# One core, a four-half-layer decoder step in split fp32: parts of the inner dimension, the order around the residual, the mean square and the block sums

## The reference, cut to what matters

```python
def rms_norm(x, g):
    y = x * lax.rsqrt(jnp.mean(x * x, axis=-1, keepdims=True) + EPS)
    return y * g

def swiglu_ffn(x, w_in, w_out):            # w_in 1024 x 5632, w_out 2816 x 1024
    gate, up = jnp.split(x @ w_in, 2, axis=-1)
    return (jax.nn.silu(gate) * up) @ w_out

for l in range(2):
    if l == 1:
        kv = rms_norm(x, kv_norm) @ w_kv   # keys (rotated) and values, kept for the attention
    x = x + 0.5 * swiglu_ffn(rms_norm(x, norm_ffn[l, 0]), ffn_w_in[l, 0], ffn_w_out[l, 0])
    h = rms_norm(x, norm_mix[l])
    mix = conv_module(h, ...) if l == 0 else diff_attention(rope(h @ w_q), ...) @ w_o
    x = x + mix
    x = x + 0.5 * swiglu_ffn(rms_norm(x, norm_ffn[l, 1]), ffn_w_in[l, 1], ffn_w_out[l, 1])
y = rms_norm(x, norm_final)
```

## Time and profile before

| | us |
|---|---|
| median of 3 runs | 2050.07 |
| the profiled execution | 2052.34 |
| its span | 2050.5 |
| TensorE matmuls (PE) busy | 1940.7 |
| VectorE (DVE) busy | 1431.8 |
| ScalarE (ACT) busy | 874.0 |
| GpSimd (POOL) busy | 332.7 |

### The profile page before, as it was taken

How to read it: one execution, slowest core, us unless ns; L and a number is a source line. 1 busy time by engine, 2 the same in 40 slices (tenths; PEclk the granted TensorE clock), 3 DMA queues, 4 the chain that set the end, 5 groups by cost and what they waited for, 6 DMA issues and landing times. The chain is left out here.

```text
span 2050.5 us, 36491 instructions
## 1 busy us (share of the span) xinstructions
PE 1940.7 (95%) x15236; PEld 1859.0 (91%) x15236; DVE 1431.8 (70%) x1775; ACT 874.0 (43%) x1259; POOL 332.7 (16%) x343
## 2 busy tenths in 40 slices
PE   4999999999798999999998999999988989999997
PEld 3999999888598999999998999999875789999996
DVE  6776768699857758667655847667678567667585
ACT  5433424455545425234234424334356454334242
POOL 1101011133111011011411111011431121011111
PEclk9999999999899999999998999999999999999998
DMA  9768585388448487682549677673677167686752
GB/s 272 166 174 224 137 216 129 88 160 170 96 144 194 117 222 168 189 192 78 151 150 225 165 190 190 166 191 103 183 230 247 45 152 188 168 205 152 204 142 64
DMA packets 318784, 340.71 MB, mean 166 GB/s; under 512 B 12163, under 2 KB 279812, under 8 KB 318476
## 3 DMA queue, kind: packets, MB, share of 16 engines
q1 hardware_dynamic: 275460, 216.97, 33.7%
q0 software_dynamic: 33840, 111.21, 28.8%
q10 hardware_dynamic: 9320, 10.20, 1.7%
HBM read 221.58 MB, written 7.53 MB: 112 GB/s over the span
## 5 line engine op out<-in xcount | busy, mean ns | idle before, releaser
L682 PE MATMUL ps_all<-xs_hi_low,w_hi 128*128 128x260 f32 x1848 | 530.4, 287 | 36.0 <-DVE w_lo L1418 21.3
L682 PE MATMUL ps_all<-xs_hi_low,w_lo 128*128 128x260 f32 x1848 | 529.0, 286 | 0.0
L682 PE MATMUL ps_all<-xs_lo_low,w_hi 128*128 128x260 f32 x1848 | 526.3, 285 | 0.0
L1017 ACT ACTIVATE w_hi<-raw 128x1024 fp32r<-128x1024 f32 (+1 forms) x252 | 259.1, 1029 | 390.1 <-PE ps_all L652 132.2
L1418 DVE TENSOR_TENSOR w_lo<-raw,w_hi 128x1024 fp32r<-128x1024 f32 (+1 forms) x252 | 311.7, 1237 | 129.9 <-ACT w_hi L1017 126.7
L682 PEld LDWEIGHTS ps_all<-xs_hi_low,w_hi 128*128 128x128 f32 x1848 | 354.3, 192 | 38.4 <-issue 25.7
L682 PEld LDWEIGHTS ps_all<-xs_lo_low,w_hi 128*128 128x128 f32 x1848 | 353.9, 191 | 0.2
L682 PEld LDWEIGHTS ps_all<-xs_hi_low,w_lo 128*128 128x128 f32 x1848 | 353.4, 191 | 0.0
L1017 ACT ACTIVATE w_hi<-raw_more_low 128x1024 fp32r<-128x1024 f32 x156 | 165.2, 1059 | 290.1 <-PE ps_all L682 184.0
L1418 DVE TENSOR_TENSOR w_lo<-raw_more_low,w_hi 128x1024 fp32r<-128x1024 f32 x156 | 192.0, 1231 | 118.4 <-ACT w_hi L1017 117.1
L652 PE MATMUL ps_all<-hs_hi_low,w_hi 128*128 128x260 f32 x1056 | 215.4, 284 | 2.8 <-DVE t_gate L1489 2.6
(11 more groups left out here) (254 smaller groups left out, 3612.2 us busy)
## 6 DMA issues: line engine op xcount, KB each, us to landing
raw_more_low<-w_in SPq DMA_DIRECT2D x105, 512.0 KB, 7.1
raw<-w_in SPq DMA_DIRECT2D x80, 512.0 KB, 6.0
raw_more_low<-raw_more_low POOLq DMA_DIRECT2D x72, 512.0 KB, 6.4
raw<-w_out SPq DMA_DIRECT2D x64, 512.0 KB, 4.2
raw<-raw POOLq DMA_DIRECT2D x60, 512.0 KB, 6.8
raw_more_high<-w_in SPq DMA_DIRECT2D x34, 512.0 KB, 6.9
raw<-w_out SPq DMA_DIRECT2D x32, 384.0 KB, 3.4
raw_more_high<-raw_more_high POOLq DMA_DIRECT2D x24, 512.0 KB, 6.7
```

The lines of the kernel that those rows point to most:

```text
L682: mm = nc.tensor.matmul(ps_all[:, bank, 0:HALF], w[:, ring, j * GW + q * P:j * GW + (q + 1) * P], m, start=j == 0 and k == 0, stop=j == PA ...
L1017: nc.scalar.activation(w_hi[:, n % RING, 0:width], src, ACT.Copy).then_inc(hi_made, 1)
```

## The change

Six things are changed.

1. `PARTS` is (6, 8, 8): the first part of each block has 3 groups and 6-tile chunks, the last one 4 groups and 8-tile chunks.
2. In the residual phases the weights of item n + 3 are made at the end of chunk n (`step(n + 1)`) and not at the start of the next one. Where pair sums are made (conv_out and o) VectorE drains x ahead of the rest of the pair before, and ScalarE squares an even tile first of all, rounds the next weights, and only then copies; at an odd tile it copies, rounds the next weights, then rounds the pair and squares.
3. The mean square of an up phase stands ahead of item 5, on banks 6 and 7, its root and refinement follow, and its result is awaited ahead of item 0 of group 1.
4. `add_pairs` adds S1 + W22 first, then S3 + W11; first loads come in the order W11, W12, S1, W22, S3.
5. In the first group of f 2 the blocks S1 and S3 have places of their own, like W12, and so wait for no free place.
6. At the start of the kernel all five blocks are loaded ahead of the constants.

```diff
-PARTS = (8, 8, 6)
-PART_AT = (0, 8, 16)
+PARTS = (6, 8, 8)
+PART_AT = (0, 6, 14)
...
-        ps_stat_up = ps_all[:, 0:2, 0:HALF]
+        ps_stat_up = ps_all[:, 6:8, 0:HALF]
...
-                for blk in (W11, W12, S3, S1, W22) if first_in else (S3, S1, W22, W11, W12):
+                for blk in (W11, W12, S1, W22, S3) if first_in else (S3, S1, W22, W11, W12):
                     s = blk + 5 * in_second(ph, g)
+                    apart = ph.f == 2 and ph.part == 0 and g == 0 and blk in APART
+                    after = 0 if apart else need[s]
...
+                    elif i == 0 and g == 1 and fresh(ph):
+                        pe.wait_ge(rstd_made, made + 1)
...
                     elif i == 5:
                         pe.wait_ge(p1_copied, ph.group0 + g + 1)
-                        if g == 0 and fresh(ph):
-                            pe.wait_ge(rstd_made, made + 1)
...
-                            if i == 3 and g == 0 and fresh(ph):
-                                variance(sums, (p1_copied, ph.group0 + 1), ps_stat_up)
+                            if i == 5 and g == 0 and fresh(ph):
+                                variance(sums, (taken, sums_of(ph, g, 3)), ps_stat_up)
...
@@ scalar, residual
+                    def square():
+                        act.wait_ge(summed, sums + m - 1)
+                        nc.scalar.activation(sq[:, m % 2, :], at(x, m), ACT.Square).then_inc(squared, 1)
+                    def following():
+                        if m < KD - 1:
+                            step(ph.chunk0 + m + 1)
...
-                        pair_hi(s, m)
...
+                        if m % 2 == 0:
+                            square()
+                            following()
+                            pair_hi(s, m)
+                        else:
+                            copy_x(s, m)
+                            following()
+                            pair_combos(s, m)
+                            square()
...
@@ vector, up
-                    if g == 0 and fresh(ph):
-                        rms(ps_stat_up)
                     thirds(g)
                     step(n + 5)
                     up_second(g)
...
+                    if g == 0 and fresh(ph):
+                        rms(ps_stat_up)
                     step(n + 6)
...
@@ vector, residual
-                    step(n)
-                    if s in (2, 6):
-                        pair_before_lo(s, m)
+                    if m == 0 or not ph.final:
+                        step(n)
...
                     if s in (2, 6):
-                        pair_sums(s, m)
+                        pair_before_lo(s, m)
+                        if m % 2:
+                            pair_sums(s, m)
+                        if m < KD - 1:
+                            step(n + 1)
+                        if m % 2 == 0:
+                            pair_sums(s, m)
+                        pair_lo(s, m)
...
@@ gpsimd
-                for to, of, done in ((S3, W11, s3_added), (S1, W22, s1_added)):
+                for to, of, done in ((S1, W22, s1_added), (S3, W11, s3_added)):
```

More of the change, by code:

```diff
@@ L262, in trunk @@
         stage_2, = over(XG + 108160, KD * T * 4, [("stage_2", [P, 8, HALF])])
-        w12_first, = over(XG + 62464, KD * P * 4, [("w12_first", [P, KD * P])])
+        first_places = over(XG + 54144, 3 * KD * P * 4, [(f"first_block{i}", [P, KD * P]) for i in range(3)])
         def stage_of(s, j):
@@ L394, in trunk @@
         W11, S1, W22, S3, W12 = range(5)
+        APART = {S1: 0, S3: 1, W12: 2}
         BLOCK_OF = (W11, W12, S3, W11, S1, W22, W12)
@@ L404, in trunk @@
                 first_in = ph.group0 + g == 0 or ph.kind == "up" and ph.f == 2 and ph.part == 0 and g == 0
-                for blk in (W11, W12, S3, S1, W22) if first_in else (S3, S1, W22, W11, W12):
+                for blk in (W11, W12, S1, W22, S3) if first_in else (S3, S1, W22, W11, W12):
                     s = blk + 5 * in_second(ph, g)
+                    apart = ph.f == 2 and ph.part == 0 and g == 0 and blk in APART
+                    after = 0 if apart else need[s]
+                    if not apart:
+                        need[s] = ph.chunk0 + ITEMS * g + FREED_BY[blk] + 1
+                    elif blk != W12:
+                        s = 10 + APART[blk]
                     filled[s] += 16
@@ L409, in trunk @@
                     a, b = {W11: (0, 0), W12: (0, 1), W22: (1, 1), S1: (1, 0), S3: (1, 0)}[blk]
-                    of_phase.append((s, need[s], ph.weights(g, a, b), g, blk))
-                    need[s] = ph.chunk0 + ITEMS * g + FREED_BY[blk] + 1
+                    of_phase.append((s, after, ph.weights(g, a, b), g, blk))
             for c in range(ph.chunks):
@@ L440, in block_of @@
         def block_of(ph, g, block):
-            if ph.f == 2 and ph.part == 0 and g == 0 and block == W12:
-                return w12_first[:, :]
+            if ph.f == 2 and ph.part == 0 and g == 0 and block in APART:
+                return first_places[APART[block]][:, :]
             return raw_of(ph, block + 5 * in_second(ph, g))
@@ L572, in _ @@
                 sp.dma_start(x[:, 2 * i:2 * i + 2, :], xT[:, 2 * i:2 * i + 2, :]).then_inc(x_in[i], 16)
-                if i < 3:
-                    load(first, i)
+                load(first, i)
+            load(first, 4)
             sp.dma_start(cst[:, :], cst_d).then_inc(inputs, 16)
@@ L577, in _ @@
             sp.dma_start(pages_s[0:1, :], pages).then_inc(inputs, 16)
-            load(first, 3)
-            load(first, 4)
             for m in range(4):
@@ L1146, in up @@
                             hidden_hi(g - 1)
-                        elif not g and i == 3 and fresh(ph):
+                        elif not g and i == 5 and fresh(ph):
                             root(ps_stat_up)
@@ L1185, in residual @@
                         continue
-                    step(ph.chunk0 + m)
-                    act.wait_ge(summed, sums + m - 1)
+                    if m == 0:
+                        step(ph.chunk0)
                     if ph.kind == "down":
```

33 lines of the change are left out of this document (16 added, 17 removed).

## The result

The changed kernel takes 2001.37 us (median, 1999.82 to 2003.08) against 2050.39 before: ratio 0.9766, 95% interval 0.9749 to 0.9783. Timed again beside later kernels it took 1999.99 us, ratio 0.9756 (0.9743 to 0.9769). So 49 us are won; the prediction was 2000, with a sum of 50.3 us against the profiled execution.

What follows compares the result with a forecast made beforehand. PE, busy 1940.7 of 2050.5 us, was taken as the bound, so only its waits and half clock could be won. Terms summed to 50.3 us off the profiled 2052.3, giving 2002.0, or 2000 us as median; range 1992 to 2013.

Steps and rivals of the forecast that it cites:

- Last down phases: Last down phases of f 0, f 1, f 2: 8-tile chunks make PE the bound, 2.7 us each, 8.1 us won.
- The ring of 5.21 us: Last down phase before: VectorE and ScalarE loop through x, copy, square, w_hi, w_lo, drain, against 4.3 us of PE.
- Squares earlier: k, q and conv_in: wait for summed squares and half clock go, 4.7 us each in k and q, 4.2 in conv_in; 13.6.
- Order in conv_out and o: New order makes PE bound the pair loop, 11.5 us for 14.11; 9.4 and 9.0 us, together 18.4.
- Mean square behind item 4: First group of f 1 and f 3: rstd wait and half clock go, 0.3 us wait stays; 3.65 each, 7.3 us.
- f 0: First group of f 0: item 5 starts behind the mean square at 48.3, not 51.36; 2 us, between -1 and 5.
- Block sums: Reordered sums, f 2's first group and later groups: item 2 needing the second sum costs 0, between -2 and 2 us.
- Tail: Kernel's end: last half chunk covers 0.7 us more of the mean square's wait, chunk 7 overlaps better; 1.4 us won.
- Even-group starts: Down phases behind a group of even count start with a 0.2 us gap, f 2 has two more; -0.5 us.
- signs of being wrong: Mean square waiting over 1 us, a pair above 12 us, or PE waiting for an added block in item 2.
- Rival 3: Half-clock stretches stay since shorter gaps still bring them, 13.6 us of the sum: 2014 us; chance 0.06.
- Rivals 1 and 2: Rival 1: pair loop finds another ring, 2009 or 2018, 0.12; rival 2: rstd or mean square late, 2011, 0.09.

Runs made afterwards that it cites:

- part-of-6 run: Kernel before with the inner tiles in parts of 6, 8, 8 and nothing else: 2030.73 us, ratio 0.9899.
- block-sum run: Kernel before with only the block sums reordered, three places of f 2's first group apart, first loads ahead of the constants: 2050.58 us, ratio 0.9993.

## Why the prediction came out

Terms of the sum, with what the traces (before against after, table above) and the single runs show:

- **Last down phases**, 8.1: 8.8. The ring of 5.21 us against 4.3 us of PE was read rightly; the first chunks cost 0.2 us, not 0.45.
- **Squares earlier**, 13.6: 4.7 in k, 5.8 in conv_in, 4.0 in q, 14.5, with some 3 us of spread in conv_in and q (4.7 and 5.3 by the changed kernel's second profile). The recorded sum has a slip: 3.1 + 0.9 for conv_in is 4.0, not 4.2. The parts alone bring them. Both terms together, 21.7: 20.7 measured (17.6 to 23.6).
- **Order in conv_out and o**, 18.4: with the mean square already moved, conv_out and f 1 go from 8.76 + 6.60 to 3.12 + 2.98 lost, o and f 3 from 9.12 + 6.74 to 3.91 + 2.68: 18.5. In the changed kernel a pair takes 11.54 us from even drain to even drain (578.59 to 590.13), as forecast, and 336 matmuls run in 40.00 us, with no idle time:

```profile
561.00:601.00 40.00, 40.00 (x336) 40.00 (x335) 32.59 (x39) 23.66 (x31) 14.61 (x12) 1.00 0.69 190
```

- **Mean square behind item 4**, 7.3 in f 1 and f 3: 6.3 alone (3.23 + 3.03), but 3.1 once the new order is there (4.38 - 2.98 and 4.34 - 2.68). The prediction gave this term all of the half clock behind rstd's wait; the order alone removes that too. Since I counted it once, the sum of both terms stands: 18.5 + 6.3 = 24.8 against 25.7. The wait that takes the old one's place was given as 0.3 us:

```profile
611.66 1.12 PE L738 MATMUL ps_all<-acc,ones_d 128*128 128x260 f32 x4 [0.27 <-DVE t_gate L1580]
```

- **f 0**, 2, between -1 and 5: 4.8, the mis-sized term. I had the mean square there at 47.3 and item 5 behind it at 48.3; the trace has 47.01 and 47.77, so item 5 starts 3.6 us earlier than at 51.36, not 3. What I left out is the clock: item 5 ran at half clock behind its old wait and took 4.48 us, and now takes 3.05. The stretch from 36 to 56 us, before and after:

```profile
36.00:56.00 20.00, 14.09 (x78) 13.53 (x79) 13.66 (x21) 9.08 (x14) 1.94 (x3) 0.74 0.89 236
```

```profile
36.00:56.00 20.00, 16.74 (x119) 16.26 (x120) 15.87 (x23) 11.11 (x15) 2.25 (x4) 0.91 0.94 237
```

  41 matmuls more in the same 20 us, 4.9 us, of which only 2.65 us are less idle time; the rest is the clock's rise from 0.74 to 0.91.

- **Block sums**, 0: 1.4 (-0.4 to 3.1) by the ratio, nothing to be told. **Tail**, 1.4: 1.1. **Even-group starts**, -0.5: f 2's first part and the gaps behind even groups take 1 to 3 us; the part-of-6 run shows 16.80 lost in f 2 and the block-sum run 16.30, the six without either, the kernel before among them, 14.9 to 15.2.

Two of the prediction's signs of being wrong did appear. The mean square waits over 1 us in f 0, 1.93 us for t_gate. And in f 2 item 2 waits for an added block, 2.09 us in this profile and 3.95 in the second one, where ScalarE's w_hi for it waits for the sum to land:

```profile
1057.39 1.06 ACT L1021 ACTIVATE w_hi<-first_block 128x1024 fp32r<-128x1024 f32 x1 [2.38 <-DMA first_block<-raw]
```

The kernel before had such a wait too (2.72 us), and the prediction priced f 2 at nothing because item 3 waits for a later sum anyway; by the table f 2's first part loses 1 to 2 us more than before. How much of that is this wait was not separated.

So the total was right at 50.3 against 49 to 52. The mechanism of the large terms was right, but that the total is so close is in part luck: the gain in f 0 was put 3 us too low, those of f 2 and the even starts 0.5 to 2.5 too high, and these nearly cancel. Rival 3, half clock staying behind shorter gaps, failed where it was tested: last down phase, conv_out from 561 to 601 and f 1 from 602 run at 1.00. Rivals 1 and 2 had 0.5 and 0.8 us of slack as their case; both slacks held, the first by the loop's 336 matmuls in 40.00 us, the second measured at about 0.75.

## What to carry to other kernels

A ring through two in-order engines is opened on the engine where the work that others wait for stands behind work that itself waits; here turning the other engine's order alone gave nothing, and its share showed only where the phase ends. When PE's pace has to be kept, size the last chunks before a reduction so that PE is the bound there: this one line of sizes gave 21 us, most of it in phases that it does not touch. And when two edits each remove a wait near one another, count the slow clock behind them once, for both.

## What the hardware showed that was not expected

- The same wait of 1.85 us is followed by a granted clock of 0.59 or of 1.00, by what PE did in the time before it (fences above). A wait's price in clock can't be read off its length alone.
- VectorE's w_lo of 1024 wide weights, usually 1.22 us, took 2.3 us six times in the changed kernel and never before. The runs with both orders have these six too, those with the parts, ScalarE's or VectorE's order alone have none. Here it stands beside GpSimd's addition of squares, which itself takes 2.00 in place of 1.3 us (two timelines, VectorE and GpSimd, of the changed kernel):

```profile
581.80 2.33 DVE L1442 TENSOR_TENSOR w_lo<-raw,w_hi 128x1024 fp32r<-128x1024 f32 x1
```

```profile
578.65 1.32 POOL L2050 TENSOR_TENSOR acc<-acc,sq 128x520 f32<-128x520 f32 x1 [6.63 <-ACT sq L1200]
...
581.05 2.00 POOL L2050 TENSOR_TENSOR acc<-acc,sq 128x520 f32<-128x520 f32 x1
```

  The Trainium skill ("SBUF — State Buffer", SBUF: two separate sides) says that the two engines share a port pair and that the loser waits for the whole instruction; 2.33 - 1.22 = 1.1 us fits that, as GpSimd's addition ends at 583.05, 1.1 us ahead of w_lo's end at 584.13. It cost nothing in the loop, where PE has no idle time. Whether tighter orders meet it more often in general was not tested.
